# Dense attention of a two-block network: score and value products as three split products, softmax's normalising pass on GpSimd

## The reference

```python
def gqa_attention(q, k, v):
    ...
    def block(qi):
        s = jnp.einsum('bkgqd,bksd->bkgqs', qi, k).astype(jnp.float32) * scale
        pr = jax.nn.softmax(s, axis=-1).astype(v.dtype)
        return jnp.einsum('bkgqs,bksd->bkgqd', pr, v)
```

## Time and profile before

| | before |
|---|---|
| median of 3 runs | 4389.39 us (4385.1 to 4394.71) |
| the profiled execution | 4390.2 us, span 4388.4 us |
| mean granted TensorE clock | 0.879 |
| PE busy | 3439.4 us, 78% |
| DVE busy | 2186.4 us, 50% |
| ACT busy | 1069.0 us, 24% |
| POOL busy | 1055.1 us, 24% |
| first attention product to last output copy | 2006.9 to 2321.3 us |

### The profile page before, as it was taken

How to read it: one execution, slowest core, us unless ns; L and a number is a source line. 1 busy time by engine, 2 the same in 40 slices (tenths; PEclk the granted TensorE clock), 3 DMA queues, 4 the chain that set the end, 5 groups by cost and what they waited for, 6 DMA issues and landing times. The chain is left out here.

```text
span 4388.4 us, 40582 instructions
## 1 busy us (share of the span) xinstructions
PE 3439.4 (78%) x15001; PEld 2526.2 (58%) x15001; DVE 2186.4 (50%) x4198; ACT 1069.0 (24%) x1934; POOL 1055.1 (24%) x865
## 2 busy tenths in 40 slices
PE   3899378668993787598998979748859477799788
PEld 2578345545783456344446857747747477688333
DVE  4599864435998653244441115237735476301112
ACT  1332044103320441123441203121122111221011
POOL 1122300331223004210004332134432354423000
PEclk9999679879996799799999989768879788899899
DMA  4023210630232104310002131022131122412310
GB/s 171 22 61 103 108 47 13 211 115 23 60 104 108 46 10 144 109 53 0 1 1 89 48 107 44 2 62 60 41 87 29 46 60 52 130 51 91 129 72 38
DMA packets 186353, 301.84 MB, mean 69 GB/s; under 512 B 38540, under 2 KB 109964, under 8 KB 182442
## 3 DMA queue, kind: packets, MB, share of 16 engines
q1 hardware_dynamic: 165036, 261.49, 19.0%
q10 hardware_dynamic: 21120, 37.76, 2.4%
HBM read 239.29 MB, written 59.90 MB: 68 GB/s over the span
## 5 line engine op out<-in xcount | busy, mean ns | idle before, releaser
L574 PE MATMUL psum<-qs,hT 128*128 128x512 f32 x1536 | 352.7, 392 | 14.2 <-POOL qs L641 14.2
L574 PEld LDWEIGHTS psum<-qs,hT 128*128 128x128 f32 x1536 | 291.1, 190 | 75.8 <-issue 15.0
L671 DVE TENSOR_SCALAR_CACHE_REDUCE junk<-score,cand 128x384 uint8<-128x384 f32 x372 | 327.4, 942 | 2.2
L1831 PE MATMUL psum<-hTs,cws 128*128 128x512 f32 x1152 | 293.0, 415 | 33.9 <-POOL hTs L1960 33.9
L1831 PEld LDWEIGHTS psum<-hTs,cws 128*128 128x128 f32 x1152 | 227.9, 201 | 91.3 <-POOL hTs L1960 33.8
L1577 PE MATMUL psum<-bhsn,bringn 128*128 128x512 f32 x1152 | 264.4, 392 | 15.5 <-POOL bringn L1622 14.7
L1577 PE MATMUL psum<-bhsa,bringa 128*128 128x512 f32 x1152 | 264.1, 392 | 9.5 <-POOL bringa L1622 9.5
L1087 PE MATMUL psum<-w_out,oys 128*128 128x512 f32 x768 | 197.0, 420 | 76.7 <-POOL oys L1123 50.5
L1577 PEld LDWEIGHTS psum<-bhsn,bringn 128*128 128x128 f32 x1152 | 217.5, 189 | 62.2 <-issue 14.9
L1577 PEld LDWEIGHTS psum<-bhsa,bringa 128*128 128x128 f32 x1152 | 218.2, 189 | 55.8 <-issue 10.3
L1087 PEld LDWEIGHTS psum<-w_out,oys 128*128 128x128 f32 x768 | 156.1, 205 | 118.4 <-POOL oys L1123 55.6
(11 more groups left out here) (372 smaller groups left out, 6682.8 us busy)
## 6 DMA issues: line engine op xcount, KB each, us to landing
stg<-in_w_in SPq DMA_DIRECT2D x80, 256.0 KB, 2.8
pj<-ptmp ACTq DMA_DIRECT2D x64, 256.0 KB, 2.1
dlb<-blocks SPq DMA_DIRECT2D x32, 512.0 KB
wa<-in_w_ada SPq DMA_DIRECT2D x8, 1536.0 KB, 7.9
wa<-in_w_ada ACTq DMA_DIRECT2D x8, 1536.0 KB, 6.1
cwst<-in_w_in SPq DMA_DIRECT2D x24, 512.0 KB, 3.9
oyf<-yTd SPq DMA_DIRECT2D x16, 512.0 KB, 6.7
ostg<-in_w_out SPq DMA_DIRECT2D x16, 512.0 KB, 4.9
```

The lines of the kernel that those rows point to most:

```text
L574: mm = pe.matmul(ps[:, m, :], lhs, rhs, start=(kc == 0 and x == 0), stop=(kc == KC - 1 and x == 2))
L671: ins = dve.tensor_scalar(junk[:, SC_OFF[b]:SC_OFF[b + 1]], spans[b], s1, 0.0, op, ALU.add, accum_out=cnt[:, b:b + 1])
L1831: mm = pe.matmul(ps[:, u % 4, :], ws[c % 2][:, a, kc, :], hs[:, b, kc, half * HALF:(half + 1) * HALF], start=(kc == 0 and x == 0), stop=(k ...
```

## The change

Both products of the stage become split products of three, and the operands are split once.

- Keys: ACT copies each key head to `aks` hi (line 1483 of the changed kernel), DVE subtracts for lo (line 1543). Values: DVE copies all 128x2048 to `avs` hi (line 1546), GpSimd makes lo (line 1508). Queries: for each group, ACT copies 128x512 to `aqs` hi (`q_hi`, line 1464) and GpSimd makes lo (`q_lo`, line 1498). The first two groups' queries are split ahead of everything; `q_hi(m+2)` and `q_lo(m+2)` stand behind the last unit of group m.
- Probabilities: ACT's copy out of PSUM (`keep_turned`, line 1479) now writes hi; DVE reads the same PSUM bank again and writes lo = PSUM - hi (`keep_low`, line 1532, two of 128x512 a unit). The transposes now wait for lo, as does `values`.
- `scores(n)` has 6 products of 128x512 instead of 2, `values(m)` 24 instead of 8, each with one record instead of two.
- Of `normalise`, DVE keeps the reciprocal (`invert`), and the pass over 1024 elements goes to GpSimd (line 1503).
- The buffer of the stage before that held the projection's input is given back before this stage, which makes room for the new tiles.

Line 1398 on, cut to its core:

```diff
             def turn(n):
...
                     if u >= 2:
-                        pe.wait_ge(s_pT, u - 1)
+                        pe.wait_ge(s_lo, u - 1)
...
             def values(m):
-
-                pe.wait_ge(s_pT, 2 * G * (m + 1))
+                pe.wait_ge(s_lo, 2 * G * (m + 1))
+                if m == 0:
+                    pe.wait_ge(s_vlo, 1)
...
                 for kb in range(NT):
-                    mm = pe.matmul(ps[:, 6 + m % 2, :], a.v[:, kb, kv * D2:(kv + 1) * D2], pT[m % 2][:, kb, :, :],
-                                   start=(kb == 0), stop=(kb == NT - 1))
+                    for x, (v, p) in enumerate(THREE):
+                        mm = pe.matmul(ps[:, 6 + m % 2, :], vs[:, v, kb, kv * D2:(kv + 1) * D2], pT[m % 2][:, p, kb, :, :],
+                                       start=(kb == 0 and x == 0), stop=(kb == NT - 1 and x == 2))
...
         @block.scalar
         def _(act):
+            def q_hi(m):
+                if m >= KVH:
+                    act.wait_ge(s_qk, G * (m - 1))
+                act.activation(qs[m % KVH][:, 0], q_tile(m), ACT.Copy).then_inc(s_qhi, 1)
...
             for n in range(N):
                 if n + 2 < N:
                     exps(n + 2)
                 keep_turned(n)
+                if n % G == G - 1 and n // G + 2 < N // G:
+                    q_hi(n // G + 2)
+
+        @block.gpsimd
+        def _(pool):
+            def q_lo(m):
+                pool.wait_ge(s_qhi, m + 1)
+                pool.tensor_tensor(qs[m % KVH][:, 1], q_tile(m), qs[m % KVH][:, 0].bitcast(F32),
+                                   ALU.subtract).then_inc(s_qlo, 1)
+
+            def normalise(n):
+                pool.wait_ge(s_ri, n + 1)
+                pool.tensor_scalar(pm[n % 3][:, :], pm[n % 3][:, :], ri[:, n:n + 1], None, ALU.mult).then_inc(s_nrm, 1)
+
+            for m in range(KVH):
+                q_lo(m)
+            pool.wait_ge(s_vhi, 1)
+            pool.tensor_tensor(vs[:, 1], a.v[:, :, :], vs[:, 0].bitcast(F32), ALU.subtract).then_inc(s_vlo, 1)
+            for n in range(N):
+                normalise(n)
+                if n % G == G - 1 and n // G + 2 < N // G:
+                    q_lo(n // G + 2)
...
+            def keep_low(n):
+                for c in range(2):
+                    dve.wait_ge(s_pT, 2 * n + c + 1)
+                    dst = pT[n // G % 2][:, :, 4 * c:4 * c + 4, n % G, :]
+                    dve.tensor_tensor(dst[:, 1], ps[:, 4 + c, :].rearrange("p (b q) -> p b q", b=4),
+                                      dst[:, 0].bitcast(F32), ALU.subtract).then_inc(s_lo, 1)
...
             for n in range(N):
-                normalise(n)
                 if n + 2 < N:
                     row_max(n + 2)
+                keep_low(n)
+                if n + 2 < N:
+                    invert(n + 2)
                 if n % G == 1 and n > G:
                     keep_out(n // G - 1)
```

More of the change, by code:

```diff
@@ L1386, in stage_dense_attention @@
     scale = float(D2 ** -0.5)
+    THREE = ((0, 0), (0, 1), (1, 0))
     with ExitStack() as ctx:
         pm = [k.sb(ctx, f"apm{i}", [P, SEQ]) for i in range(3)]
-        pT = [k.sb(ctx, f"apT{i}", [P, NT, G, P]) for i in range(2)]
+        pT = [k.sb(ctx, f"apT{i}", [P, 2, NT, G, P], F32R) for i in range(2)]
+        qs = [k.sb(ctx, f"aqs{i}", [P, 2, G, P], F32R) for i in range(KVH)]
+        ks = k.sb(ctx, "aks", [P, 2, KVH, SEQ], F32R)
+        vs = k.sb(ctx, "avs", [P, 2, NT, KVH * D2], F32R)
         mx = k.sb(ctx, "amx", [P, N])
@@ L1393, in stage_dense_attention, with q_tile @@
         ri = k.sb(ctx, "ari", [P, N])
-        s_qk, s_nm, s_exp, s_nrm, s_T, s_pT, s_pv, s_o, s_ch = (k.sem(n) for n in (
-            "scores", "neg_max", "exps", "normed", "turned", "pT_kept", "values", "out", "dve_chain"))
+        s_qk, s_nm, s_exp, s_ri, s_nrm, s_T, s_pT, s_lo, s_pv, s_o, s_ch = (k.sem(n) for n in (
+            "scores", "neg_max", "exps", "inverse_sums", "normed", "turned", "pT_hi", "pT_lo", "values", "out",
+            "dve_chain"))
+        s_qhi, s_qlo, s_khi, s_klo, s_vhi, s_vlo = (k.sem(n) for n in (
+            "q_hi", "q_lo", "k_hi", "k_lo", "v_hi", "v_lo"))
         block = ctx.enter_context(nc.Block())
+        def q_tile(m):
+            i, kv = divmod(m, KVH)
+            return a.qT[:, kv * G:(kv + 1) * G, i * P:(i + 1) * P]
         @block.tensor
@@ L1400, in scores @@
             def scores(n):
-                i, hd = divmod(n, QH)
+                m, j = divmod(n, G)
+                kv = m % KVH
+                if n < QH and j == 0:
+                    pe.wait_ge(s_klo, kv + 1)
+                if j == 0:
+                    pe.wait_ge(s_qlo, m + 1)
                 if n >= 2:
@@ L1404, in scores @@
                 for c in range(2):
-                    mm = pe.matmul(ps[:, 2 * (n % 2) + c, :], a.qT[:, hd, i * P:(i + 1) * P],
-                                   a.kT[:, hd // G, c * HALF:(c + 1) * HALF], start=True, stop=True)
+                    for x, (q, kk) in enumerate(THREE):
+                        mm = pe.matmul(ps[:, 2 * (n % 2) + c, :], qs[kv][:, q, j, :],
+                                       ks[:, kk, kv, c * HALF:(c + 1) * HALF], start=(x == 0), stop=(x == 2))
                 mm.then_inc(s_qk, 1)
@@ L1455, in keep_turned @@
                     act.wait_ge(s_T, 2 * n + c + 1)
[L1456 removed]
+                    act.activation(pT[n // G % 2][:, 0, 4 * c:4 * c + 4, n % G, :],
                                    ps[:, 4 + c, :].rearrange("p (b q) -> p b q", b=4), ACT.Copy).then_inc(s_pT, 1)
+            for m in range(KVH):
+                act.activation(ks[:, 0, m, :], a.kT[:, m, :], ACT.Copy).then_inc(s_khi, 1)
+                q_hi(m)
             exps(0)
@@ L1485, in keep_out @@
                                 ps[:, 6 + m % 2, :].rearrange("p (h q) -> p h q", h=G)).then_inc(s_o, 1)
+            for m in range(KVH):
+                dve.wait_ge(s_khi, m + 1)
+                dve.tensor_tensor(ks[:, 1, m, :], a.kT[:, m, :], ks[:, 0, m, :].bitcast(F32),
+                                  ALU.subtract).then_inc(s_klo, 1)
             row_max(0)
+            dve.tensor_copy(vs[:, 0], a.v[:, :, :]).then_inc(s_vhi, 1)
             row_max(1)
+            invert(0)
+            invert(1)
             for n in range(N):
-                normalise(n)
                 if n + 2 < N:
                     row_max(n + 2)
+                keep_low(n)
+                if n + 2 < N:
+                    invert(n + 2)
                 if n % G == 1 and n > G:
@@ L2829, in second_block @@
             a.v = k.sb(qkv, "v2", [P, NT, KVH * D2])
-            stage_attention_inputs(k, hT, a)
+            with ExitStack() as projecting:
+                hT = k.sb(projecting, "h2T", [P, KC, SEQ])
+                stage_attention_inputs(k, hT, a)
             stage_dense_attention(k, a)
```

6 lines of the change are left out of this document (2 added, 4 removed).

## The result

The changed kernel takes 4524.98 us (median of 4 runs, 4523.14 to 4526.38) against 4390.93 us for the kernel before on the same chip (4 runs). The ratio is 1.0306, 95% interval 1.0288 to 1.0324. The forecast was 4509 us, range 4455 to 4538. The profiled execution took 4523.14 us, with a span of 4521.2 us, where the one before took 4390.2 us. The stage now runs from 2006.8 to 2452.5 us, so it is 131 us longer; what is behind it is as long as it was, within 2 us.

A forecast was written before the change was run, and what follows sets the result against it. PE was taken to bound the stage. Groups growing from 19.1 to 27.0 us give +103, the last period +2.7, start +15, end -1: 120 us on 4390.2, set to 4509 us against the median; range 4455 to 4538.

The forecast's parts named there:

- rival 2: POOL's normalising pass costs 2.4 us, making each long step's transposes 1.3 us later: 4520 to 4527 us; chance 0.12.
- Short step: Time between successive row maxima without a value burst, all in series through DVE and ACT: 4.6 us.
- POOL's queue: POOL's query low part, queued ahead of the normalising pass, ends 1.1 us into the long step, delaying the transposes.
- long step: Row maximum to row maximum with transposes, 24 value products and scores on PE between: 9.9 us before the clock's cost.
- POOL's pass: POOL's normalising pass over 1024 elements, for which the transposes wait: taken as 1.1 us, upper end 2.4 us.
- The clock: PE's clock falls after a 4.9 us pause in every group, costing 2.7 us; a group takes 27.0 us.
- the 0.8 that I had named as a sign: Granted PE clock of the stage in the changed profile should be about 0.8.
- Stage start and end: Start: splitting operands first delays unit 7's row maximum, 15 us more; end: shorter last value product saves about 1 us.
- Rival 1: PE's clock does not fall; a period is 24.4 us and the time 4472 us; chance 0.13.
- Rival 3: POOL's queue is not late; long step 7.5 us, period 21.9 us, +53, time 4443 us; chance 0.10.
- Rival 4: A split product on PE costs 0.43 instead of 0.225 us; period 32 us, time near 4590 us; chance 0.05.
- Rival 5: DVE and ACT chain not in series, PE sets the pace, short step under 3.6 us; about 4361 us; chance 0.03.

The follow-up runs named there:

- run 2: Changed kernel with POOL's query low part moved behind, instead of ahead of, the first normalising pass of the group before it: 4450.95 us, ratio 1.0144.
- run 6: Changed kernel with POOL's normalising pass over only 384 of 1024 elements, the rest left unnormalised: 4503.32 us, ratio 1.0273.
- run 3: Changed kernel with 24 extra products, result overwritten, filling PE's pause ahead of the transposes of each long step: 4506.65 us, ratio 1.0270.
- run 8: On top of run 2's move, ScalarE copies unit n out of PSUM ahead of the exponentials of unit n+2: 4369.6 us, ratio 0.9967.
- run 1: Changed kernel with the normalising pass back on VectorE, split products kept, POOL keeping only the query and value low parts: 4474.25 us, ratio 1.0199.
- run 4: Kernel before the change, products unsplit, with only the normalising pass moved to POOL: 4459.95 us, ratio 1.0167.

## Why the prediction held, point by point

**The range, the sign and the place of the cost were right.** The time lies in the range, 16 us above the forecast, on rival 2's side. All of the time comes from the stage (131 of 133 us between the two profiled executions), as in the sum.

**Short step:** forecast 4.6 us, measured 4.43. From the row maximum to the exponentials it is 1.43 us, to the first copy 1.10, to the first low part 0.62, and the two low parts and the reciprocal take 1.28; I had 1.32 for the low parts alone and 0.15 for signals on top. That is about 0.5 us a group too much.

**POOL's queue:** the instruction ends 1.0 us into the long step (forecast 1.1), and run 2 shows that it cost 69 us together with what followed from it.

**POOL's pass was the mis-sized term.** The forecast said: "I take 1.1 us, because the pass has a single input of that length like the memset": it takes 2.85 us, above even my upper end of 2.375 us, a pass with two inputs over as many elements. The memset has no input, and the one-column pass says nothing about the price of further columns; no row of the trace of before had a GpSimd pass with a per-partition factor over a long row, and the nearest of the two ends was the upper one. By run 6 the true price is worth 17 us against a pass of 1.25 us. The Trainium skill, page "GPSIMD Engine Reference", section "Engine selection", grants an operation with one input roughly line rate; the trace disagrees, 2.85 us for 1024 elements against 0.753 on VectorE, a factor of 3.8. Its advice not to put such a pass there was right, and more so than its numbers.

**The clock:** it falls in each long step, as forecast, with the transposes in 1.97 us. But it costs about 1.7 us a group (run 3) and not 2.7. Since POOL's pass ended later than I had thought, the work at the lower level was a smaller part of the burst. Run 6 shows this: with a pass of 1.25 us the clock costs 2.4 us a group on average, near the 2.7. The stage's mean clock was 0.86, not the 0.8 that I had named as a sign. The two errors offset each other: 2.85 - 1.1 = 1.75 us more for the pass, about 1 us less for the clock and 0.5 less for the short steps give 27.2 against the forecast 27.0; measured 27.3. They belong together, since the longer pass made the clock's part smaller, but I had not foreseen it. That my group was right to 1% is therefore partly luck, and run 6 shows nearly the forecast's own case, a pass of 1.25 us: +117 us, where I had put +120.

**Stage start and end:** 15 us were forecast for the start. The late row maximum of unit 7 is at

```profile
2054.85 1.23 DVE L1520 TENSOR_REDUCE amx<-psum 128x1 f32<-128x1024 f32 x1 [6.33 <-PE psum L1421]
```

48.0 us behind the moment at which PE had started before (2006.88), against 30.3: 17.7 us. The row maximum of unit 3 is 1.8 us later than forecast, and the first long step takes 13.6 us instead of 12.5. At the end I had expected 1 us less and got 2 us more, since the last two turns wait for POOL and the last values begin at the lower clock. The end of the stage, to set beside the earlier trace rows:

```profile
2433.21 1.23 DVE L1520 TENSOR_REDUCE amx<-psum 128x1 f32<-128x1024 f32 x1 [4.69 <-PE psum L1421]
...
2444.12 7.22 PEld L1445 LDWEIGHTS psum<-apT,avs 128*128 128x128 f32 x24 [1.81 <-DVE apT L1532]
...
2451.80 0.69 DVE L1538 COPY attT<-psum 128x512 f32<-128x512 f32 x1 [7.74 <-PE psum L1445]
```

From the last row maximum to the last copy it is 19.3 us, before it was 17.1. Summed: 17.7 + 111.3 for the fourteen groups between + 2.2 = 131.2 us, against 15 + 105.7 - 1 = 120.

**Rivals.** Rival 2 (POOL's pass at 2.4 us, 4520 to 4527 us) had the right mechanism with a price still too low, and its number. Rival 1, no fall of the clock, is out: the transposes take 1.97 us in every long step with a wait for POOL. Rival 3's long step of 7.5 us is what run 2 showed in six of fifteen groups (7.6 us); its 4443 us (+53) stand beside +65. Rival 4, a split product of 0.43 us, is out by run 3's 24 in 5.73 us. Rival 5, the faster case, needed the copies ahead of the exponentials; run 8 built that, and its condition was right (short steps under 3.6 us), while the value burst kept it at 4370 us.

**What is not additive:** the splits without the pass on POOL cost 88.5 us (run 1), the pass on POOL without the splits 74 us (run 4), both together 134 us.

**What stays open:** why the clock falls inside the burst in nine of run 2's fifteen groups and not in the other six. How much of run 2's 69 us is the turn's earlier start and how much the clock is an estimate; no run separates them.

## What to carry to other kernels

Less work on the busiest engine gave nothing here as long as its burst, its queue order and the two engines that take turns stood in series around it; with the same instructions the kernel is 134 us slower than before in one order and 62 us faster in another. Look at which unit's operation stands ahead of which on every in-order engine, GpSimd's too: one subtraction of 1.26 us ahead of the wrong pass cost 69 us, and a reciprocal behind the wrong row maximum cost 66. Cut a burst into as many parts as there are steps to hide it in before making it shorter.

## What the runs showed of the hardware that I had not expected

GpSimd's multiplication by one factor for each partition takes 2.842 to 2.862 us for 1024 float32 elements and 1.25 us for 384, which is 2.5 ns an element, more than a multiplication of two tensors of the same length (2.375 us).

VectorE and GpSimd get in each other's way at some operations. The start of the changed stage, where both subtract one SBUF tensor from another (line 1543 on VectorE, 1498 on POOL):

```profile
2007.85 1.23 DVE L1543 TENSOR_TENSOR aks<-k2T,aks 128x1024 fp32r<-128x1024 f32 x1 [5.21 <-ACT aks L1483]
...
2008.42 4.01 POOL L1498 TENSOR_TENSOR aqs<-q2T,aqs 128x512 fp32r<-128x512 f32 x2 [8.63 <-ACT aqs L1464]
...
2009.32 1.97 DVE L1543 TENSOR_TENSOR aks<-k2T,aks 128x1024 fp32r<-128x1024 f32 x1 [0.24 <-ACT aks L1483]
```

VectorE's second key subtraction takes 1.97 us and its first, which had begun before POOL's, 1.23; POOL's two take 4.01 us, and one alone 1.26. In run 1 the pass on VectorE took 1.47 us beside the same subtraction instead of 0.76. The low part that VectorE makes from a PSUM and an SBUF tensor is not slowed: two take 1.29 us at 2167.55 of the changed kernel, where POOL rests, and 1.29 us at 2132.09 in run 2, where POOL's pass (2129.96 to 2132.81) lies beside the first of them. This agrees with the Trainium skill, page "GPSIMD Engine Reference", section "Specifications", which has GpSimd share its SBUF interface with VectorE and names as the cases of contention VectorE's instructions with two SBUF inputs or in a mode that uses two ports. Whether VectorE's pass, which has one SBUF input, is of the second kind, no run here shows. In the changed kernel I see it only at the start of the stage, where POOL's two subtractions take 1.5 us more than twice 1.26; by my estimate it is about 1 us of the 17.7.
